# Seven changes of order in a two-block transformer kernel on one core: the eighth head's norm, silus, paired panels, one-hots behind panels, fetches, residual sums and the staging place of the first logits

## The reference

```python
# first block, one layer
ada = silu(c) @ ada_w + ada_b                      # shifts, scales and gates
u = rms_norm(h, norm1_g) * (1 + sc1) + sh1
zq, zf, zi, zg, zca, zcb, zga, zgb = split(u @ w_in)
o = hgrn2_chunkwise(q, 1 - f, i, log f)            # 8 heads of 128, gated linear attention
o = rms_norm(o, hg_norm_g) per head
y_a = (o * silu(zg)) @ w_a
cv = causal_depthwise_conv(zca * sigmoid(zcb), conv_w, conv_b)   # 31 taps
y_b = silu(layer_norm(cv)) @ w_b
h = h + g1 * ((sigmoid(zga) * y_a + sigmoid(zgb) * y_b) @ w_out)
u2 = rms_norm(h, norm2_g) * (1 + sc2) + sh2
h = h + g2 * peer(u2)      # 8 heads pick 16 of 128 x 128 experts from two lists of scores, gelu
h = rms_norm(h, final_g)
# second block: windowed attention A + mlp, then differential attention B + mlp
h = h + attention_A(rms_norm(h));  h = h + relu(rms_norm(h) @ w_in)**2 @ w_out
h = h + attention_B(rms_norm(h));  h = h + relu(rms_norm(h) @ w_in)**2 @ w_out
out = rms_norm(h, norm_final_g)
```

## Time and profile before

| what | value |
|---|---|
| median of 3 runs | 3836.3 us (3835.07 to 3838.34) |
| profiled execution | 3836.27 us, its span 3834.5 us |
| mean granted clock of TensorE | 0.98 |
| VectorE busy | 2330.4 us |
| ScalarE busy | 1313.5 us |
| GpSimd busy | 1488.1 us |
| a panel's high part on ScalarE, mean | 1.06 us |
| a panel's low part on GpSimd, mean | 2.49 us |

### The profile page before, as it was taken

How to read it: one execution, slowest core, us unless ns; L and a number is a source line. 1 busy time by engine, 2 the same in 40 slices (tenths; PEclk the granted TensorE clock), 3 DMA queues, 4 the chain that set the end, 5 groups by cost and what they waited for, 6 DMA issues and landing times.

```text
span 3834.5 us, 48650 instructions
## 1 busy us (share of the span) xinstructions
PE 3683.7 (96%) x16460; PEld 2918.2 (76%) x16460; DVE 2330.4 (61%) x3639; ACT 1313.5 (34%) x1802; POOL 1488.1 (39%) x684
## 2 busy tenths in 40 slices
PE   6999899899999999999999999999999999999998
PEld 4787787688888888878888887865688877358886
DVE  5786997145767575268888885336574431658541
ACT  4554323334443434321111112236422232653221
POOL 2211443333333333344444443454244444124442
PEclk8999999999999999999999999989999999899999
DMA  5435222233555464676555552221122223212222
GB/s 201 149 109 193 94 92 82 83 96 115 162 160 177 145 190 136 214 241 198 185 183 183 184 188 97 94 73 48 59 96 95 98 88 97 63 45 94 94 95 82
DMA packets 267075, 486.58 MB, mean 127 GB/s; under 512 B 16770, under 2 KB 148226, under 8 KB 266658
## 3 DMA queue, kind: packets, MB, share of 16 engines
q1 hardware_dynamic: 90816, 304.12, 24.2%
q10 hardware_dynamic: 176132, 180.76, 14.5%
HBM read 415.48 MB, written 84.02 MB: 130 GB/s over the span
## 4 chain that ended last, share of the span: by engine, by line
PE 90%; DVE 3%; ACT 3%; issue 2%; DMA 1%; POOL 1%; DVEq 0%; SPq 0%; ACTq 0%; POOLq 0%
PE ps L376 26%; PE ps L377 26%; PE ps L378 26%; PE ps L598 3%; PE ps L697 2%; DMA ring<-panels 1%; PE ps L473 1%; PE ps L675 1%; PE ps L409 1%; PE ps L687 1%; PE ps L679 1%; ACT arena L1213 0%; PE ps L578 0%; PE ps L404 0%; ACT arena L1219 0%
## 5 line engine op out<-in xcount | busy, mean ns | idle before, releaser
L1968 POOL TENSOR_TENSOR ring_r<-ring,high_w 128x1024 fp32r<-128x1024 f32 x552 | 1371.9, 2487 | 2083.8 <-ACT high_w L796 1607.9
L376 PE MATMUL ps<-uT_r,high_w 128*128 128x512 f32 x2624 | 1048.4, 400 | 23.4 <-POOL ring_r L1968 10.2
L378 PE MATMUL ps<-uT_r,ring_r 128*128 128x512 f32 x2624 | 1027.9, 392 | 0.0
L796 ACT ACTIVATE high_w<-ring 128x1024 fp32r<-128x1024 f32 x440 | 464.3, 1058 | 1283.6 <-PE ps L378 1125.9
L377 PE MATMUL ps<-sq_r,high_w 128*128 128x512 f32 x2048 | 800.2, 391 | 0.0
L377 PE MATMUL ps<-part,high_w 128*128 128x512 f32 x1856 | 735.6, 396 | 0.0
L376 PE MATMUL ps<-part,high_w 128*128 128x512 f32 x1664 | 670.6, 403 | 11.5 <-issue 7.1
L378 PE MATMUL ps<-part,ring_r 128*128 128x512 f32 x1664 | 659.1, 396 | 0.0
L376 PEld LDWEIGHTS ps<-uT_r,high_w 128*128 128x128 f32 x2624 | 497.2, 189 | 131.2 <-issue 20.1
L378 PEld LDWEIGHTS ps<-uT_r,ring_r 128*128 128x128 f32 x2624 | 496.0, 189 | 104.4
L1364 DVE SCALAR_TENSOR_TENSOR part<-arena 128x512 fp32r<-128x512 f32 x192 | 461.9, 2406 | 6.6
(11 more groups left out here) (302 smaller groups left out, 3794.0 us busy)
## 6 DMA issues: line engine op xcount, KB each, us to landing
ring<-panels SPq DMA_DIRECT2D x568, 512.0 KB, 3.4
gdram<-arena ACTq DMA_DIRECT2D x16, 2048.0 KB, 10.7
arena<-adram ACTq DMA_DIRECT2D x128, 256.0 KB, 2.7
adram<-act_out ACTq DMA_DIRECT2D x112, 256.0 KB, 3.9
arena<-gdram ACTq DMA_DIRECT2D x112, 256.0 KB, 4.8
arena<-ada_rest ACTq DMA_DIRECT2D x32, 512.0 KB, 4.3
strips_dram<-btab ACTq DMA_DIRECT2D x4, 3584.0 KB
arena<-strips_dram ACTq DMA_DIRECT2D x32, 448.0 KB, 3.3
```

The source lines that it names most:

```text
L376: t_.matmul(out, wh, xh, start=(k == 0), stop=False)
L378: last = t_.matmul(out, wl, xh, start=False, stop=(k == KT - 1))
L796: s_.activation(high_w[:, j % RING], ring[:, j % RING], ACT.Copy).then_inc(hi_ready, 1)
L1968: g_.tensor_tensor(ring_r[:, j], ring[:, j], high_w[:, j], ALU.subtract).then_inc(lo_ready, 1)
```

## The change

a. *Eighth head's norm.* ScalarE runs Ln and Exp of head 7 behind gate pair 0, VectorE the head's mean ahead of and its gate behind convolution pair 0 (which is taken out of the loop). GpSimd makes the low parts of four more panels before it waits for the first `og` tile. The gate's sigmoid goes to `sg[:, 1]`.
b. *Silus and paired Wb.* ScalarE's last high part in Wa comes behind silu 2, VectorE's low parts of the convolution come in turns with the scalings, and TensorE computes panels 0 and 1 of Wb slice by slice together.
c. *Norm 1 and paired Wq.* The low parts come two scalings behind, and panels 0 and 1 of Wq are paired in the same way.
d. *One-hots behind panels.* Each round has the panel first; ScalarE has the Gelu first.
e. *Fetches.* Fetches 4 to 7 of the first group are issued behind Gelus 11, 12 and 13 instead of 13 and 14.
f. *Residual sums.* The sum of squares of tile 0 goes from behind panel 2 to behind panel 3 of Wo in attention B.
g. *First logits' staging place.* The first two heads are staged in `between_r`, 2560 free columns of the arena, behind the low part of Wo's panel 0.

```diff
@@ TensorE
+            def two_panels(q8, x, ready):
+                for j in range(2):
+                    start_panel(q8, j, True)
+                xh, xl = x
+                for k in range(KT):
+                    pe.wait_ge(ready[0], ready[1] + k + 1)
+                    for j in range(2):
+                        ...   # the three matmuls of panel j, slice k
-            for j in range(KT):
-                panel(Q_WB, j, (cvh, cv_r), ready=None if j else (in_ready, 0))
+            two_panels(Q_WB, (cvh, cv_r), (in_ready, 0))
+            for j in range(2, KT):
+                panel(Q_WB, j, (cvh, cv_r))
...
-            for j in range(16):
-                panel(Q_WQ + j // 8, j % 8, (uT_r, sq_r), ready=None if j else normed(1))
+            two_panels(Q_WQ, (uT_r, sq_r), normed(1))
+            for j in range(2, 16):
+                panel(Q_WQ + j // 8, j % 8, (uT_r, sq_r))
...
                     for j in range(4):
+                        panel(c + (2 * Q_PEER + PER_TILE * tt + 3), j, (uT_r, sq_r), unit=4)
                         for par in range(2):
...
-                        panel(c + (2 * Q_PEER + PER_TILE * tt + 3), j, (uT_r, sq_r), unit=4)
...
+                    if s and j in (2, 3):
+                        for n in () if j == 2 else (2, 3):
+                            behind(6, n)
+                    else:
+                        behind(4 if s == 0 else 6, j)
@@ ScalarE
-            head_log(7)
-            head_root(7)
...
-                    s_.activation(sg[:, 0, :], ps[:, 0, :], ACT.Sigmoid).then_inc(bank_free[0], 1)
+                    s_.activation(sg[:, 1, :], ps[:, 0, :], ACT.Sigmoid).then_inc(bank_free[0], 1)
...
             gates_pair(0)
+            head_log(7)
+            head_root(7)
...
-            for j in range(4, 8):
+            for j in range(4, 7):
...
                 if k:
                     conv_high(k - 1)
+                if k == 2:
+                    taken(Q_WA, 7)
+                    high(Q_WA, 10)
...
                     for j in range(4):
+                        early(tt * PER_TILE + c + 3, j)
                         for par in range(2):
...
-                        early(tt * PER_TILE + c + 3, j)
...
-                if n >= 13:
-                    for j in ((4, 5), (6, 7), ())[n - 13]:
+                if n >= 11:
+                    for j in ((4,), (5,), (6, 7), (), ())[n - 11]:
                         fetch(0, j)
@@ VectorE
                 for k in range(KT):
                     scaled(r, k, gain)
+                    if r in SPLIT_NORM and k >= 2:
+                        low_x_of(r, k - 2)
...
-            head_mean(7)
-            head_gate(7, 1)
...
+            head_mean(7)
+            conv_pair(0)
+            head_gate(7, 1)
+            with S.loop(KT // 2 - 1, 2 * CONV_K) as i:
+                conv_pair(i + 1)
...
-                if k % 2:
-                    gated(4 + k // 2)
+                if k in (0, 1, 5, 7):
+                    gated({0: 4, 1: 5, 5: 6, 7: 7}[k])
+                if k >= 2:
+                    conv_low(k - 2)
+            for k in range(KT - 2, KT):
+                conv_low(k)
@@ GpSimd
-                po.wait_ge(lo_ready, 8 * (Q_WO_A - Q_HEADS) + RING - 1)
-                po.wait_ge(gemm_done, 8 * Q_WO_A)
-                stage_halves(a, 0)
                 for b in range(BANKS):
                     po.wait_ge(bank_free[b], 2 * Q_WO_A)
                 po.wait_ge(vt_sb, 8)
                 stage_v(a, 0)
+                po.wait_ge(lo_ready, 8 * (Q_WO_A - Q_HEADS) + RING - 1)
                 stage_halves(a, 1)
...
+            for j in range(RING):
+                low(at_gates, j)
             for k in range(KT):
                 for j in range(RING):
-                    low(at_gates + k, j)
-                po.wait_ge(og_high, k + 1)
-                g_.tensor_tensor(og_r[:, k, :], og[:, k, :], sq_r[:, k, :], ALU.subtract).then_inc(og_low, 1)
+                    if j == 2:
+                        po.wait_ge(og_high, k + 1)
+                        g_.tensor_tensor(og_r[:, k, :], og[:, k, :], sq_r[:, k, :], ALU.subtract).then_inc(og_low, 1)
+                    low(at_gates + 1 + k, j)
...
             for j in range(RING - 1):
                 low(at_a, j)
+                if j == 0:
+                    po.wait_ge(lo_ready, 8 * (Q_WO_A - Q_HEADS) + 1)
+                    po.wait_ge(bank_free[0], 2 * Q_QKV_A + 3)
+                    stage_halves(att[0], 0)
             first_attention()
```

More of the change, by code:

```diff
@@ L160, in build @@
         parts = [sb(f"part{n}", [P, KT, T], F32R) for n in range(4)]
-        sb("between", [P, 20000 - 4 * KT * T])
+        between_r = sb("between", [P, 20000 - 4 * KT * T], F32R)
         part_x = sb("part_x", [P, KT, T], F32R)
@@ L241, in build @@
         ks = sq[:, 5:7, :]
+        staged_0 = [between_r[:, T * n:T * n + T] for n in range(5)]
         staged_in = [[uT_r[:, n, :] for n in range(5)], [uT_r[:, 5, :], uT_r[:, 6, :], uT_r[:, 7, :], sq_r[:, 3, :], sq_r[:, 4, :]]]
@@ L382, in panel @@
                     last.then_inc(gemm_done, 1)
+            def two_panels(q8, x, ready):
[5 more added lines that the diff above has]
+                    for j in range(2):
+                        out = ps[:, j, :]
+                        t_.matmul(out, high_w[:, j, k, :], xh[:, k, :], start=(k == 0), stop=False)
+                        t_.matmul(out, high_w[:, j, k, :], xl[:, k, :], start=False, stop=False)
+                        ins = t_.matmul(out, ring_r[:, j, k, :], xh[:, k, :], start=False, stop=(k == KT - 1))
+                        if k == KT - 1:
+                            ins.then_inc(gemm_done, 1)
             def stat(idx, tiles, ready, at):
@@ L676, in logit @@
                     else:
-                        q2, k2, kl = staged_in[par][hh], staged_in[par][2 + hh], staged_in[par][4]
+                        to = staged_0 if isinstance(n, int) and n == 0 else staged_in[par]
+                        q2, k2, kl = to[hh], to[2 + hh], to[4]
                         t_.matmul(ps[:, qt, :], q2[:, qt * P:(qt + 1) * P], k2, start=True, stop=False)
@@ L767, in attention @@
                     panel(q_wo, j, (kT_r, qT_r), ready=None if j else (a["oT_ready"], 0), ks=some)
-                    behind(4 if s == 0 else 6, j)
+                    if s and j in (2, 3):
[3 more added lines that the diff above has]
+                        behind(4 if s == 0 else 6, j)
             attention(0, 3, Q_QKV_A, Q_WO_A)
@@ L1370, in scaled, with low_x_of @@
                                         in1=rstd[:], op0=ALU.mult, op1=ALU.mult).then_inc(upre if r in SPLIT_NORM else u_ready, 1)
+            def low_x_of(r, k):
+                ve.wait_ge(x_high, KT * SPLIT_NORM[r] + k + 1)
+                v_.scalar_tensor_tensor(out=(sq_r if r else ulo)[:, k, :], in0=sq[:, k, :],
+                                        scalar=ada[:, 24 * r + k:24 * r + k + 1], in1=uT_r[:, k, :],
+                                        op0=ALU.add, op1=ALU.subtract).then_inc(u_ready, 1)
             def low_x(r):
                 for k in range(KT):
-                    ve.wait_ge(x_high, KT * SPLIT_NORM[r] + k + 1)
-                    v_.scalar_tensor_tensor(out=(sq_r if r else ulo)[:, k, :], in0=sq[:, k, :],
-                                            scalar=ada[:, 24 * r + k:24 * r + k + 1], in1=uT_r[:, k, :],
-                                            op0=ALU.add, op1=ALU.subtract).then_inc(u_ready, 1)
+                    low_x_of(r, k)
             GAIN = {4: "mlp0", 5: "mix1", 6: "mlp1"}
@@ L1605, in _, with conv_pair @@
             ada_out(5, 5)
-            head_mean(7)
-            head_gate(7, 1)
             PAD = CONV_K - 1
             S.done(v_.memset(glu[:, 0:PAD], 0.0))
-            with S.loop(KT // 2, 2 * CONV_K) as i:
+            def conv_pair(i):
                 q8 = i + Q_GATES
@@ L1654, in _ @@
                                         op0=ALU.mult, op1=ALU.mult).then_inc(cvn_ready, 1)
-                if k % 2:
-                    gated(4 + k // 2)
-            for k in range(KT):
-                ve.wait_ge(cv_high, k + 1)
-                v_.tensor_tensor(cv_r[:, k, :], cv[:, k, :], cvh[:, k, :], ALU.subtract).then_inc(in_ready, 1)
+                if k in (0, 1, 5, 7):
+                    gated({0: 4, 1: 5, 5: 6, 7: 7}[k])
+                if k >= 2:
+                    conv_low(k - 2)
+            for k in range(KT - 2, KT):
+                conv_low(k)
             for j in range(KT):
@@ L2054, in _ @@
                     low(i, j)
+            for j in range(RING):
+                low(at_gates, j)
             for k in range(KT):
                 for j in range(RING):
-                    low(at_gates + k, j)
-                po.wait_ge(og_high, k + 1)
-                g_.tensor_tensor(og_r[:, k, :], og[:, k, :], sq_r[:, k, :], ALU.subtract).then_inc(og_low, 1)
+                    if j == 2:
+                        po.wait_ge(og_high, k + 1)
```

(10 more changed lines are left out.)

11 lines of the change are left out of this document (7 added, 4 removed).

## The result

The changed kernel took 3790.4 us (median of four runs, 3788.4 to 3795.4) and the kernel before, on the same chip, 3835.7: a ratio of 0.9883, 95% interval 0.9869 to 0.9896. Forecast were 3790 and a range of 3777 to 3809. The profiled execution of after is the longest of its four, 3795.39 with a span of 3793.6. Against the span of before it gains 40.9 us where the medians differ by 45.3; where the missing 4.4 lie is part of what follows.

The account below looks back on a forecast made before the run. The tensor engine was taken as the bound, busy 3683.7 us of a 3834.5 us span, with seven stalls to shorten. Terms 7.4 + 5.5 + 3.5 + 19.3 + 3.4 + 3.0 + 4.8 = 46.9 off 3836.3 gave 3790, range 3777 to 3809.

Parts of the forecast that it names:

- a, 7.4: Eighth head's norm: tensor engine resumes 9.5 us earlier, but the convolution bounds the stage; gain 7.4 us, bounds 6 and 12.
- R2: Rival: convolution no bound at the eighth head's norm, clock never falls at three other stalls; 3779 us, chance 0.10.
- b, 5.5: Silus and paired Wb: both panels end 6.3 us earlier, then gated sums are late; gain 5.5 us, bounds 3 and 8.
- c, 3.5: Norm 1 and paired Wq: engine resumes at 722.0 at 1.2 GHz; gain 3.5 us, bounds 2 and 5.6.
- d, 19.3: One-hots behind panels: 12.9 us of waits and 8.0 of clock and issue go; gain 19.3 us, bounds 10 and 20.9.
- The cover is gone exactly: One-hot loop: next tile's selection would have no slack before the transposes; 0.5 us charged at each of three boundaries.
- R1: Rival: selection becomes the wait in the one-hot loop through more GpSimd holds; 3802 us, chance 0.13 with milder forms.
- R3: Rival: reordered one-hot rounds exceed 7.24 us; an overrun of 1 us gives 3854 us, chance 0.03.
- e, 3.4: Fetches before the first down panel: eight activation tiles run on without the 3.37 us wait; gain 3.4, bounds 1.3 and 6.
- f, 3.0: Residual sums: Wo's panel 3 goes first, starting 2.8 us earlier, probably at higher clock; gain 3.0 us, bounds 2 and 5.
- g, 4.8: First logits: bias strip lands in about 3.7 us, first unit starts near 2540.2, not 2545.00; gain 4.8, bounds 3 and 8.
- R4: Rival: each stall has a second cause as late as the first; 3817 us, or 3836 with the one-hots; chance 0.08.

Follow-up runs that it names:

- e_again: The changed kernel run and profiled once more with no edit: median 3794.0 us against 3837.3 for the kernel before, ratio 0.9884.
- e_no_holds: The changed kernel with twelve low parts made by ScalarE as plain copies instead of GpSimd's subtraction: median 3786.6 us, 49.2 under the kernel before.
- e_no_b: The changed kernel with only the silu order and paired Wb panels put back: median 40.3 us under the kernel before.

## Why the prediction was right, step by step

The total was right (3790 against 3790.4 and, in the second comparison, 3794.0), and its largest term was right with its mechanism. Predicted 46.9; 45.3 by the medians, and the profile pair has 40.9, of which the seven columns make 40.1. "Measured" is the column of after, "undone" what the profile without the edit has less in the same column.

- **What bounds it: right.** All seven places gave time. Nothing between them moved in the changed kernel.
- **a, 7.4; measured 6.1, undone 5.8.** Right with both bounds: the engine resumed at 386.49 after 0.70 us idle, and waited at the last conv mean. That mean began 7.8 us earlier, counted from ahead of a, where 7.4 was forecast. Two errors cancelled in it. The head's gate, "I take 3.9", took 5.6 us (430.57 to 436.17), since one step of 0.75 met a low part and took 2.77. And "nothing between" the channels was wrong: 22.67 us a channel held waits of 0.2 to 0.7, which the first pair, taken out of the loop, no longer has (22.0 a channel, 1.7 us less for the pair). What made the term too large was the clock behind the new wait, put at nothing: it took 1.7 back (granted 0.78). In e_again the gate met two low parts (6.7 us), the clock stayed full behind the mean, and 6.5 is left. The new idle was 3.3 us, under the 4 to 5 named as its sign. R2 (no bound) is refuted.
- **b, 5.5; measured 4.8, in the other profiles 4.7 to 5.3, undone 5.4 or more: right**, with two small waits of 1.4 and 0.2 at the paired panels as foreseen.
- **c, 3.5; measured 3.0**, undone 1.9 to 3.3. The engine resumed at 710.43; with the 11.6 us gained ahead of it that is 3.3 sooner than 725.34, as forecast. Idle 6.6 for 9.9, the clock at half pace behind it as assumed.
- **d, 19.3; measured 20.9 by the trace, undone 20.8, and 20.5 by the medians.** The waits are gone, and so are the 8.0 of clock and issue. The charge of 0.5 us at three boundaries was wrong: "The cover is gone exactly" assumed that the selection takes 69.2 us whatever stands beside it. Windows over it, last one-hot to last slot, of before and then of after:

```profile
1010.17:1079.35 69.18, 69.18 (x315) 57.60 (x314) 65.84 (x207) 22.07 (x28) 33.06 (x12) 1.00 0.79 252
```

```profile
994.38:1058.48 64.10, 64.10 (x292) 53.37 (x292) 60.76 (x207) 20.53 (x26) 28.19 (x11) 1.00 0.82 263
```

The same 207 instructions took 5.1 us less, beside 11 low parts instead of 12, and all of it lies in three of them: a cast from 2.03 to 0.29 us, and two products of 128x2048 from 4.37 and 3.56 to 2.29 each. One line of such products, two in the stretch (count, ns min/median/max), of before and then of after:

```profile
L1716 DVE TENSOR_TENSOR arena<-arena x2: 4367/4368/4368, 1060.8 to 1071.1; 128x2048 f32<-128x2048 f32 x2
```

```profile
L1762 DVE TENSOR_TENSOR arena<-arena x2: 2292/3329/4366, 1043.3 to 1050.2; 128x2048 f32<-128x2048 f32 x2
```

The slots were ready 4.9 us ahead of the transposes, nearly the old 5.2. R1 is refuted, and by what its "for" named: holds decide, and they became fewer. Every round of the 64 behind the first of its tile starts 7.24 us after the one ahead, as before, so R3 is refuted. The window over one of them:

```profile
900.00:907.24 7.24, 7.24 (x42) 6.29 (x41) 3.85 (x7) 3.49 (x4) 2.41 (x1) 1.00 0.33 109
```

- **e, 3.4; measured 0.8, undone 1.4: the step that failed.** "All eight tiles run on" was right, "1672.25 - 3.37" wasn't: the tiles moved into the time of a fifth low part, against four in before, 3.37 - 2.1 = 1.3, and they took 27.1 us instead of 28.4. They also began 1 us sooner against the tensor engine, so its idle fell by 2.2 us, and the slower return of the clock, which the sum left out, took more than half of that back (granted 0.68 over 10.7 us). The other sum, that by the rule of the Trainium skill (SBUF — State Buffer, section "SBUF: two separate sides"), was the better one, though it counted a third low part where there was a fifth; here the trace and e_no_holds agree with the rule, 2.1 us a hold and none without GpSimd.
- **f, 3.0; measured 2.4, in six other profiles 3.8 to 4.0;** with the edit undone 0.7 is lost. Right: the panel waits 2.2 us for its low part. Whether the clock falls on that wait decided between the two values; "probably at the higher clock" was true in six profiles with the edit and false in six.
- **g, 4.8; measured 2.1 in the profile pair, 3.8 to 6.6 elsewhere,** by the medians 2.4. The logits themselves went 6.2 us sooner, as forecast. The unit behind them came 3.1 us sooner, not 4.8: "lands in about 3.7 us" was the misjudged step. The strip landed 5.1 us behind its issue and the unit began 5.4 behind it; the same strip had taken 4.2 in before, and only in e_no_b did it take 3.7. So the unit came 6.2 us behind the last value copy, not the 4 to 5 named as the sign.
- **The sum.** That it hit the median to 0.4 us is in part luck. In the profile pair a, b, c, e, f and g came out smaller by 1.3, 0.7, 0.5, 2.6, 0.6 and 2.7 and d larger by 1.6, 6.8 us short in all; the changed kernel's other runs were shorter than its profiled one, and the clock at B and clock and strip at g move a run by as much as these errors. The upper bounds of the seven terms add up to 65.5 us and so to 3771, not to the 3773 of the text, which changes nothing in the range. R4 (a second cause as late as the first) came near in e, and in part in g.

## What to carry to other kernels

Where a matrix engine waits for something that was built just before, put a piece of independent work of the same engine between: in d it gave back the waits and, with 8 of 20.8 us, the clock and issue behind them. Before you count an engine's work as fixed, ask what runs beside it on the engine with which it shares its way to memory: in d and e it was holds of 2.1 us, met or missed, that set the size, and in a one more was hidden by a second error. And a gain under 3 us in a stretch of short waits is better read from the same instruction's start in several traces, not from medians that the clock moves by more.

## What the runs showed of the hardware that was not expected

- In these two lines holds go by the operands. Views of two lines of the vector engine in after (count, min/median/max in ns): the split's product of SBUF tiles alone takes 2.77 us in more than half of 192 cases, the convolution's, with one operand and the result in PSUM, never more than 0.76 in 224, though GpSimd made low parts beside both.

```profile
L1391 DVE SCALAR_TENSOR_TENSOR part<-arena x192: 691/2771/2800, 1608.1 to 3687.1; 128x512 fp32r<-128x512 f32 x192
```

```profile
L1665 DVE SCALAR_TENSOR_TENSOR ps<-arena,cc,ps x224: 744/751/764, 388.6 to 569.4; 128x512 f32<-128x512 f32 x112
```

- A hold can hide a transfer: in e_no_holds fetch waits of 0.5, 2.5 and 1.4 us came out when 10.3 us of holds were gone.
- The same code at the same place runs at 0.54 or at 1.00 of the clock in two executions (B above). Behind the same wait of 0.70 us ahead of the first gate panel it was 1.00 in after and, as the second window has it, 0.64 in e_again. By the last conv mean both wait 3.2 us for the vector engine, so there it costs nothing (a is -6.1 and -6.5).

```profile
386.30:391.00 4.70, 4.51 (x20) 3.77 (x21) 4.66 (x8) 2.49 (x5) 3.42 (x2) 1.00 0.51 208
```

```profile
386.30:391.00 4.70, 4.00 (x11) 3.13 (x11) 4.46 (x7) 3.07 (x6) 2.83 (x2) 0.64 0.51 210
```
